# Reordering the key-side pipeline of a streaming-encoder block, with square root and reciprocal apart and fixed engines for its copies

## The reference

```python
xn = rms_norm(h, norm1_g)
z_a, q, c_kv, q_idx, k_idx, w_idx, gates = split(xn @ w_in)
y_a = spatial_gating_unit(gelu(z_a), ...)             # gMLP branch
y_b = indexer_sparse_attention(q, rms_norm(c_kv, kv_norm_g),
                               q_idx, k_idx, w_idx, w_uk, w_uv)
mixed = g_a * (y_a @ w_oa) + g_b * (y_b @ w_ob)       # g = sigmoid(gates)
h = h + mixed @ w_out
hn = rms_norm(h, norm2_g)
h = h + (silu(hn @ w_ff_gate) * (hn @ w_ff_up)) @ w_ff_down
out = rms_norm(h, final_g)
```

## Time and profile before

| | |
|---|---|
| runs, median (lowest to highest) | 3922.43 us (3920.58 to 3924.27) |
| profiled execution, its own time | 3925.11 us |
| its span, slowest core (core 1) | 3924.0 us |
| spans of the eight cores | 3894.3 to 3924.0 us |
| mean granted TensorE clock, all cores | 0.908 to 0.911 |
| busy share PE, DVE, ACT, POOL | 78%, 38%, 30%, 4% |
| key stage, 0 to 357 us: PE, DVE, ACT busy | 209.3, 133.0, 133.0 us |
| own rows' front, 357 to 420 us: PE busy, clock | 15.7 us, 0.50 |
| rest, 420 to 3924 us: PE busy | 2851.5 us |

### The profile page before, as it was taken

One profiled execution on the slowest core, in us unless ns is written; L12 is line 12 of the kernel. 1 busy time (PEld: TensorE's weight loads), 2 busy tenths in 40 slices (PEclk: granted clock), 3 DMA queues, 4 the chain that ended last, 5 costly groups with the idle time before them and its releaser, 6 DMA issues.

```text
span 3924.0 us, 51307 instructions; the slowest of 8 cores (3894.3 to 3924.0 us)
## 1 busy us (share of the span) xinstructions
PE 3076.4 (78%) x17936; PEld 1506.5 (38%) x17936; DVE 1498.2 (38%) x2394; ACT 1172.9 (30%) x2038; POOL 150.2 (4%) x144
## 2 busy tenths in 40 slices
PE   3665667777038888888896619999888999999996
PEld 2333311111015555555543214444344444444442
DVE  2443278899954444444400341111122021110204
ACT  3343167777115555555512110000021000000001
POOL 0000000000000000000000000000000000000000
PEclk9887788888569999999998759999998999999998
DMA  6334200000011111111457336664483555466543
GB/s 169 107 108 108 25 1 1 1 1 1 0 16 18 18 18 18 18 18 21 72 69 107 43 45 85 86 77 52 85 151 43 75 76 66 69 87 91 76 65 107
DMA packets 263370, 224.93 MB, mean 57 GB/s; under 512 B 10064, under 2 KB 251728, under 8 KB 256208
## 3 DMA queue, kind: packets, MB, share of 16 engines
q0 software_dynamic: 250304, 156.08, 30.4%
q1 hardware_dynamic: 12816, 65.56, 5.2%
HBM read 369.31 MB, written 8.39 MB: 96 GB/s over the span
## 4 chain that ended last, share of the span: by engine, by line
PE 62%; DVE 22%; issue 6%; ACT 4%; DMA 4%; DVEq 1%; ACTq 0%; SPq 0%; POOL 0%; POOLq 0%
PE ps L241 61%; DVE arena L255 11%; DVE arena L263 5%; ACT arena L247 3%; DVE arena L259 3%; DMA arena<-w_in 3%; PE ps L244 1%; DVE arena L253 1%; ACT arena L267 1%; DVE arena L251 1%; DMA arena<-w_out 1%; DVEq L143 1%; DMA arena<-x_all 1%; DVE arena L543 0%; DVE arena L540 0%
## 5 line engine op out<-in xcount | busy, mean ns | idle before, releaser
L241 PE MATMUL ps<-arena 128*128 128x512 bf16 (+3 forms) x16768 | 2987.9, 331 | 344.6 <-DVE arena L263 179.4
L241 PEld LDWEIGHTS ps<-arena 128*128 128x128 bf16 x16768 | 1421.7, 99 | 1889.8 <-issue 790.4
L247 ACT ACTIVATE arena<-ps 128x512 bf16<-128x512 f32 (+1 forms) x824 | 469.8, 596 | 1574.1 <-PE ps L241 1564.1
L263 DVE TENSOR_TENSOR arena<-ps,arena 128x512 f32<-128x512 f32 (+1 forms) x344 | 237.9, 692 | 1287.1 <-PE ps L241 1257.7
L244 PE MATMUL ps<-identb,arena 128*128 128x128 bf16 x1168 | 127.4, 258 | 469.6 <-DVE arena L259 225.4
L255 DVE TENSOR_SCALAR_CACHE_REDUCE arena<-arena 128x512 bf16<-128x512 f32 (+7 forms) x160 | 418.0, 2612 | 19.3
L263 DVE TENSOR_TENSOR arena<-arena 128x512 bf16<-128x512 bf16 (+5 forms) x682 | 330.0, 488 | 129.1 <-PE ps L241 59.2
L247 ACT ACTIVATE arena<-ps,arena 128x512 bf16<-128x512 f32 x576 | 339.3, 736 | 22.1 <-PE ps L241 22.0
L244 PEld LDWEIGHTS ps<-identb,arena 128*128 128x128 bf16 x1168 | 96.0, 117 | 493.8 <-issue 487.2
L267 ACT COPY arena<-ps 128x128 bf16<-128x128 bf16 (+3 forms) x248 | 131.4, 530 | 421.9 <-PE ps L244 383.1
L269 DVE CAST arena<-ps 128x512 bf16<-128x512 f32 x156 | 108.0, 692 | 356.0 <-PE ps L241 356.0
(11 more groups left out here) (30 smaller groups left out, 243.9 us busy)
## 6 DMA issues: line engine op xcount, KB each, us to landing
arena<-x_all SPq DMA_DIRECT2D x32, 1024.0 KB, 6.3
arena<-w_in POOLq DMA_DIRECT2D x15, 2048.0 KB, 18.7
arena<-w_in POOLq DMA_DIRECT2D x24, 1024.0 KB, 20.4
arena<-w_ff_gate POOLq DMA_DIRECT2D x22, 1024.0 KB, 10.9
arena<-w_ff_up POOLq DMA_DIRECT2D x22, 1024.0 KB, 12.1
arena<-w_ff_down POOLq DMA_DIRECT2D x12, 1536.0 KB, 17.3
arena<-x_own SPq DMA_DIRECT2D x8, 1024.0 KB, 5.9
arena<-w_oa POOLq DMA_DIRECT2D x8, 1024.0 KB, 11.4
```

The source lines that it names most:

```text
L241: P.op("pe", lambda e: e.matmul(out, lhsT=lhsT, rhs=rhs, start=start, stop=stop), reads, writes)
L247: P.op("act", lambda e: e.activation(out=out, in_=in_, func=func, **kw), reads, writes)
L263: P.op(eng, lambda e: e.tensor_tensor(out=out, in0=in0, in1=in1, op=op), reads, writes)
```

## The change

In the key stage:

- The statistics of x are made one step earlier in the list: `k_stats_emit(g+2)` at the end of iteration g issues loads, squares and square roots. The square root takes the scale and the constant itself, so the multiply-add on DVE goes away. The reciprocals come apart, in `k_recip`, on DVE in the middle of the next iteration.
- Within an iteration the order of the steps changes from P C F for each tile to P0 C0 P1 C1 F0 P2 C2 F1 P3 C3 F2 F3 (P `post_tile`, C `back_ckv`, F `front_tile`).
- The engines of the copies are fixed: half 0 of `front_tile` on ScalarE and half 1 on DVE, `kx` and `cT` on DVE. After the stage `front_tile` uses the rotation again.

In the feed-forward part the matmuls of a 512-row half name only the four tiles of `hnT` in that half.

```diff
--- before.py
+++ after.py
@@ -358,6 +358,8 @@
     ldw(Wk[:, :, 576:640], win[:, :, C_KI:C_KI + 64], ("Wk", 2))
     WKK = [("Wk", 0), ("Wk", 1), ("Wk", 2)]
 
+    front_evac = [None, None]
+
     def front_pre(src_d, row0, ss_ap, rs_ap, sbase):
         for tt_ in range(4):
             ld(xt[tt_], src_d[row0 + tt_ * 128: row0 + (tt_ + 1) * 128, :], ("xt%d" % tt_,))
@@ -383,7 +385,7 @@
             tr(psb[kc // 8][:, (kc % 8) * 128:(kc % 8 + 1) * 128], xn[s][:, kc * 128:(kc + 1) * 128],
                [("xn%d" % s,)], [PSK[kc // 8]])
         for half in range(2):
-            cp(evac_rot.next(), dst_fn(tt_, half),
+            cp(front_evac[half] if front_evac[0] else evac_rot.next(), dst_fn(tt_, half),
                psb[half][:, 0:1024].rearrange("p (a b) -> p a b", a=8), [PSK[half]], [dkey_fn(tt_)])
 
     def front(src_d, row0, ss_ap, rs_ap, sbase, gkey_fn, dst_fn, dkey_fn, gbc, gbckey):
@@ -409,7 +411,7 @@
         for kc in range(16):
             mm(ps[7][:, :], Wk[:, kc, 512:640], xg[gs][:, kc, :], kc == 0, kc == 15,
                [("xg%d" % gs, t4) for t4 in range(4)] + WKK, [PSK[7]])
-        cp(evac_rot.next(), kx[:, g * 512:(g + 1) * 512], ps[7][:, :], [PSK[7]], [("kx", g)])
+        cp("dve", kx[:, g * 512:(g + 1) * 512], ps[7][:, :], [PSK[7]], [("kx", g)])
         return rkey
 
     def post_tile(g, tt_, rkey):
@@ -420,28 +422,63 @@
             [PSK[b], rkey, ("kvg",)], [("cn%d" % s,)])
         for cc in range(4):
             tr(psb[6][:, cc * 128:(cc + 1) * 128], cn[s][:, cc * 128:(cc + 1) * 128], [("cn%d" % s,)], [PSK[6]])
-        cp(evac_rot.next(), cT[:, :, T * 128:(T + 1) * 128],
+        cp("dve", cT[:, :, T * 128:(T + 1) * 128],
            psb[6][:, 0:512].rearrange("p (a b) -> p a b", a=4), [PSK[6]], [("cT", g)])
 
     def kdst(gs):
         return (lambda tt_, half: xg[gs][:, half * 8:(half + 1) * 8, tt_ * 128:(tt_ + 1) * 128],
                 lambda tt_: ("xg%d" % gs, tt_))
 
-    d0, k0_ = kdst(0)
-    front(x_all, 0, ssK, rsK, 0, None, d0, k0_, g1, ("g1",))
+    def k_stats_emit(g):
+        for tt_ in range(4):
+            ld(xt[tt_], x_all[(4 * g + tt_) * 128:(4 * g + tt_ + 1) * 128, :], ("xt%d" % tt_,))
+        for hf in range(2):
+            for tt_ in (2 * hf, 2 * hf + 1):
+                c_ = 4 * g + tt_
+                act(sqj, xt[tt_], AF.Square, [("xt%d" % tt_,), ("sm", "acc")], [("sqj",), ("sm", "ss", id(ssK), c_)],
+                    accum_out=ssK[:, c_:c_ + 1])
+            c0 = 4 * g + 2 * hf
+            act(rsK[:, c0:c0 + 2], ssK[:, c0:c0 + 2], AF.Sqrt, [("sm", "ss", id(ssK), c0 + k) for k in range(2)],
+                [("sm", "rs", id(rsK), c0)], scale=1.0 / 2048, bias=EPS)
+
+    def k_recip(g):
+        keys = []
+        for hf in range(2):
+            c0 = 4 * g + 2 * hf
+            key = ("sm", "rs", id(rsK), c0)
+            P.op("dve", lambda e, c0=c0: e.reciprocal(out=rsK[:, c0:c0 + 2], in_=rsK[:, c0:c0 + 2]), [key], [key])
+            keys.append(key)
+        return keys
+
+    front_evac[0], front_evac[1] = "act", "dve"
+    k_stats_emit(0)
+    rk = k_recip(0)
+    d1, k1 = kdst(0)
+    for tt_ in range(4):
+        front_tile(tt_, rsK, 0, rk, d1, k1, g1, ("g1",))
+    k_stats_emit(1)
     for g in range(9):
         prk = post_pre(g - 1) if g >= 1 else None
-        rk = None
-        if g + 1 < 8:
-            d1, k1 = kdst((g + 1) % 2)
-            rk = front_pre(x_all, (g + 1) * 512, ssK, rsK, 4 * (g + 1))
-        for tt_ in range(4):
+
+        def Pt(tt_):
             if g >= 1:
                 post_tile(g - 1, tt_, prk)
+
+        def Ct(tt_):
             if g < 8:
                 back_ckv(g, tt_)
+
+        def Ft(tt_):
             if g + 1 < 8:
                 front_tile(tt_, rsK, 4 * (g + 1), rk, d1, k1, g1, ("g1",))
+        Pt(0); Ct(0); Pt(1); Ct(1)
+        if g + 1 < 8:
+            rk = k_recip(g + 1)
+            d1, k1 = kdst((g + 1) % 2)
+        Ft(0); Pt(2); Ct(2); Ft(1); Pt(3); Ct(3); Ft(2); Ft(3)
+        if g + 2 < 8:
+            k_stats_emit(g + 2)
+    front_evac[0], front_evac[1] = None, None
 
     dbg("cT", cT, [("cT", g) for g in range(8)], [4, 4096], BF16)
     dbg("kx", kx, [("kx", g) for g in range(8)], [4096], BF16)
@@ -888,12 +925,12 @@
                     tsl = slice(th * 512, (th + 1) * 512)
                     for kc in range(16):
                         mm(ps[bG][:, :], WG[s][:, kc, c * 128:(c + 1) * 128], hnT[:, kc, tsl], kc == 0, kc == 15,
-                           [("WG%d" % s,)] + HN, [PSK[bG]])
+                           [("WG%d" % s,)] + HN[4 * th:4 * th + 4], [PSK[bG]])
                     q = sgr.next()
                     act(sgf[q], ps[bG][:, :], AF.Silu, [PSK[bG]], [("sgf%d" % q,)])
                     for kc in range(16):
                         mm(ps[bU][:, :], WU[s][:, kc, c * 128:(c + 1) * 128], hnT[:, kc, tsl], kc == 0, kc == 15,
-                           [("WU%d" % s,)] + HN, [PSK[bU]])
+                           [("WU%d" % s,)] + HN[4 * th:4 * th + 4], [PSK[bU]])
                     tt(actT[:, fl, tsl], ps[bU][:, :], sgf[q], ALU.mult, [PSK[bU], ("sgf%d" % q,)], [("actT", fl, th)])
             pidx += 1
         f0 = (pidx - npan) * 2
```

## The result

The changed kernel takes 1.0026 of the time of the kernel before, 95% interval 1.0019 to 1.0033: 10 us slower (7 to 13), medians 3932.7 and 3922.7. Executions in which one die was slowed as a whole are left out, here and in all ratios. The forecast was 3928, 5.6 us slower: the sign is right, the time lies in the range, and the size of the loss is about half of the measured one. The profiled execution took 3931.78, its slowest core (core 7) 3930.7 us.

What follows compares the result with a forecast made beforehand. No engine always busy; the key stage's chain of waits, with a ScalarE boundary between groups, was taken as the bound. Terms 6.5 - 3.2 + 5 - 1.8 - 1.4 = +5 us on the median 3922.43 gave 3928 us, range 3908 to 3946.

Steps and rivals of the forecast that it cites:

- The boundary: Key stage, between groups: ScalarE's squares and queued latent root still hold P0, 11.4 us behind F3's transposes.
- Rival 4: Key stage: squares overlap the previous group's tail and the boundary goes, 47 us less, 3881; chance 5%.
- The period: Key stage, P0 to P0 of the next group: 42.5 us against 41.14, +1.3 for each of five, +6.5 us.
- The clock term: Key stage, Cs behind 2.45 us TensorE gaps may run at 1.2 GHz: 1.6 us a period, half taken, 0.8.
- Rivals 1 and 2: Key-stage clock: 1, stays up over the boundary, 3911, 15%; 2, falls mid-group at C2 and C3, 3942, 25%.
- First boundary: Key stage, into group 1: F3's transposes stay, P0 comes at 91.3 instead of 94.55, -3.2 us.
- Group 6 to 7: Key stage, boundary without squares: K's copy ahead of P0 makes it longer, +4.4, with the clock +5 us.
- Group 8: Key stage's end: four P in a row with copies on DVE, squares running beside on ScalarE, -1.8 us.
- Feed-forward: First feed-forward matmuls: the last wait for the copies, 1.37 us, goes, -1.4 us.
- The signs: Changed profile: P0 near 91, period near 42, F-to-P handoffs 2.6, group 7 later, no gap before feed-forward matmuls.
- rival 3: Key stage: x loads taking over 8.1 us delay each boundary; at 10 us, 12 more, 3940; chance 5%.
- The bias: New square roots carry the constant as bias: a few tenths at most per boundary; about 1 us by the skill's 93 ns.

Runs made afterwards that it cites:

- e1: Changed kernel with the latent statistics (multiply-add, root, reciprocal) listed ahead of the squares of the next x group: ratio 0.9913 to before, period 34.94 us.
- e2: Changed kernel with the copies' engines taken from the rotation again, new order and split statistics kept: ratio 0.9995 to before, period 39.93 us.
- e3: Kernel before with the statistics part alone, old order, rotating engines and old feed-forward keys: ratio 0.9981 to before, period 39.55 us.
- e4: Kernel before with the new order of steps alone, statistics in the old place, rotating engines: ratio 1.0056 to before, period 41.88 us.
- e9: Kernel before with the feed-forward keys alone, key-stage instructions unchanged: ratio 0.9995 to before, period 40.39 us.
- e7: Kernel before with the fixed copy engines alone, old order and old statistics: ratio 1.0020 to before, period 41.12 us.
- e5: Changed kernel with a key of its own for each half of a transposed x tile: ratio 0.9941 to before, period 38.64 us.
- e6: Changed kernel with DVE's copy of the index keys moved from ahead of P0 to behind C1's issue: ratio 1.0022 to before, period 42.75 us.
- e10: Changed kernel with the edits of e1 and e5 together: ratio 0.9845 to before, period 30.89 us.
- e12: The kernel of e11 run again to get an interval: ratio 0.9626 to the kernel before.
- e8: Changed kernel with e1 and e5 plus a pipelined key stage (tiles scaled early, index-key matmuls between F2 and F3): ratio 0.9695 to before.
- e11: e8 with own rows and normalised rows also scaled ahead of copies, two more PSUM banks for the second: 3766.5 us in its profiled execution.

## Why the prediction was right, and where it was off

- **The boundary** was read rightly and is the heart of it. F3's transposes to P0 were forecast at 11.4 and are 76.76 to 88.36 = 11.6; e1 shows the queued root to be the cause. Rival 4, that the boundary goes, was refuted for this change and became true for the most part with one move, worth 7.4 a period. TensorE's idle stretch in it was forecast at 7.9 and is 5.66 to 6.67, since K ran partly at 1.2 GHz where the sum had it at 2.4; that cost nothing, as P0 doesn't wait for K here.
- **The period** was forecast at 42.5 and is 42.37. The terms inside: fixed engines 2.44 (e2, reckoned 2.2), statistics -1.45 (e3), order +0.9 (e4, reckoned 1). They sum to 1.9 and not to the 1.37 of the change, and e3 and e4 have the 0.6 of scatter that e9 shows, so the parts are known to about that.
- **The clock term** was mis-sized. I put 0.8 a period for Cs behind the 2.45 us gaps. In core 7's trace two of these twelve Cs ran partly at 1.2 GHz (5.30 instead of 3.62), 17 of 96 on all cores, about 0.6 a period. That the forecast took half of the five in nine was a guess with a reason, and its landing near is in part luck: e7 has such gaps and hardly a slow C. Rivals 1 and 2 both fail, as the first C of groups 1 to 6 is slow on every core (4.6 to 6.2 from its start to the next step's, instead of 3.46) and the later ones mostly aren't. The rest of my sum was 0.1 too short.
- **The ends.** First boundary: -3.2 forecast, -4.2 measured as a mean over the cores (first scaling of group 1 to P0: 34.1, now 29.9); where the further 1.0 comes from, no run isolates. Group 6 to 7: +5 forecast, P0 to P0 went from 31.7 to 37.3. Group 8: -1.8 forecast, from P0 of group 7 to the own rows 34.7 became 32.7. The start, ahead of all this, has no term in the sum: the first scaling of group 1 comes 1.0 earlier (60.6, now 59.6), as it does in the other runs with the new statistics (e1, e2, e3, e5, e6 and e10, 59.0 to 59.6) and not in those without (e4, e7 and e9, 60.3 to 60.6). Feed-forward: -1.4 forecast, 0.9 found: the step named all of the wait as going, and missed PSUM bank 0, which ScalarE still reads for the last tile.
- **The sum.** The stage's terms give +6.2, forecast +6.5; with the feed-forward edit +5.3, forecast +5, and with the start +4.3. The whole kernel lost 10 (7 to 13). The missing 3 to 9 us stay open, and there are two places for them. One is the stage itself: its +6.2 is the difference of two single profiles, and against e9's trace of the same old instructions it is +9.8. The other is what comes behind it, where the change has no instruction but the feed-forward keys. In the single profiles the attention part (from the load of `w_uk` to the first load of the gMLP branch behind it, 819.3 before, 822.1 after, means over the cores) and all that follows it (1961.6 and 1957.7) differ by a few us both ways, and over e1 to e7, e9 and e10 what follows varies from 1951 to 1967 with nearly identical instructions; e4 and e7 too lost more in time than in the stage, e3 gained less. None of my runs tells the two apart.
- **The signs.** P0 to P0 near 42, K's copy and the wait for ScalarE ahead of P0, and handoffs of about 2.6 (on core 7 from 99.61 to VectorE's next scaling at 102.12 = 2.51) came as said; squares start 2.0 behind F3's transposes instead of 1.7. P0 of group 1 was said to be near 91, from 94.55, and is at 89.4 as a mean, from 94.7. Group 7 begins at 338.5 as a mean, from 331.4, later as said. The gap ahead of the feed-forward matmuls didn't go: 0.51 is left.
- **x arriving late** (rival 3) didn't happen: 5.0 us to landing in the median, and over the whole stage ScalarE's squares waited 5.0 us for loads of x (5.1 before).
- **The bias.** The Trainium skill, "ScalarE: Activation LUTs", section "What ACT_TABLE_LOAD costs", has about 93 ns for a pointer operand. The two-element roots with the constant take 204 ns on average here against 203 without: no such cost in this trace, and the measurement decides. Whether the constant reaches ScalarE as a pointer operand, no run here shows.

## What to carry to other kernels

Before moving work earlier on an engine that runs in order, ask what now stands behind it, and who waits for that: here a 0.2 us root behind four squares cost 7.4 us a group, and moving it took the changed kernel from 1.0026 to 0.9913 of the time before, 1.1%. A handoff between two engines that only a key asks for is paid at each use, and a copy taken out of one wait has to be followed to the next thing that is late on its engine (e6). For a change confined to a stage, compare the stage on all cores: in the changed kernel its period is the same on all cores to 0.13 us, where their whole spans differ by 33. But profile the baseline twice: in the old order two profiles of the same stage differ by 0.6 a period.

## What the runs showed of the hardware

Without gaps on TensorE, the key stage wasn't always granted full speed. In e12 two cores of one die (cores 4 to 7) ran the same stretch of it differently; windows from 80 to 200 us, first core 6, then core 4 (columns: window, length, busy PE, PEld, DVE, ACT, POOL, granted clock, DMA share, GB/s):

```profile
80.00:200.00 120.00, 120.00 (x729) 63.67 (x728) 77.38 (x98) 69.57 (x105) 0.00 (x0) 0.81 0.43 150
```

```profile
80.00:200.00 120.00, 116.28 (x836) 64.57 (x850) 88.88 (x112) 78.59 (x119) 0.00 (x0) 1.00 0.60 185
```

At a granted clock of 0.81 (neither the 1.2 nor the 2.4 GHz of the other traces) a C takes 4.37 instead of 3.62 and the period is 26.3 instead of 22.6, and its own rows begin 30 us later. Core 7 did the same and cores 0 to 5 didn't; e8's profile has it on the same two cores. The Trainium skill, "TensorE: Matmul & The Clock Gate", Part 1, describes a limit of 13/16 that takes the whole die once three of its cores run dense matmuls. These rows have that ratio (0.81), but not on the whole die: cores 4 and 5 were granted 1.00. In e11, the same kernel as e12, all eight periods are 22.60, and the profiled kernels with gaps have none so slowed (before: 40.5 to 41.2). So part of what closing the gaps gains can be taken back. That the closed gaps bring it on is a guess from few profiles, and not shown.
